# A decoder step on one Trainium2 core: order of the feed-forward groups, queue of the raw weight tiles, and order of VectorE's work at openings

## The reference, cut to what matters

```python
D_MODEL = 1024
D_FF = -(-8 * D_MODEL // (3 * 256)) * 256      # 2816

def swiglu(xn, w_gu, w_down):
    g, u = jnp.split(xn @ w_gu, 2, axis=-1)
    return (jax.nn.silu(g) * u) @ w_down

hp = hp + swiglu(rmsnorm(hp, g_ffn[l]), w_gu[l], w_down[l])
hs = hs + swiglu(rmsnorm(hs, g_ffn[l]), w_gu[l], w_down[l])
y_prompt = rmsnorm(hp, g_final)
```

## Time and profile before

| | us |
|---|---|
| median of three runs (lowest, highest) | 2819.61 (2816.98, 2821.58) |
| the profiled execution | 2815.63 |
| its span in the profile | 2813.8 |
| TensorE busy | 2749.6 (98%) |
| VectorE busy | 1560.3 (55%) |
| ScalarE busy | 1033.0 (37%) |
| GpSimd busy | 381.0 (14%) |

### The profile page before, as it was taken

One profiled execution on the slowest core, in us unless ns is written; L12 is line 12 of the kernel. 1 busy time (PEld: TensorE's weight loads), 2 busy tenths in 40 slices (PEclk: granted clock), 3 DMA queues, 4 the chain that ended last, 5 costly groups with the idle time before them and its releaser, 6 DMA issues.

```text
span 2813.8 us, 42434 instructions
## 1 busy us (share of the span) xinstructions
PE 2749.6 (98%) x16279; PEld 2630.7 (93%) x16279; DVE 1560.3 (55%) x3052; ACT 1033.0 (37%) x2222; POOL 381.0 (14%) x347
## 2 busy tenths in 40 slices
PE   8999999999999999999999999999999999999998
PEld 8788879999998999999899999999999999999998
DVE  6634653346545445545474886876555536656354
ACT  6543443233223344344343444453222323222223
POOL 2744530000000000000001330310000011000001
PEclk9999999999999999999999999999999999999999
DMA  7987759767976888798776667687664577755753
GB/s 265 353 332 280 284 189 335 259 252 268 334 303 254 328 331 313 284 376 316 284 274 243 249 239 282 242 300 247 225 240 171 196 252 274 260 198 173 254 184 116
DMA packets 203567, 742.82 MB, mean 264 GB/s; under 512 B 22732, under 2 KB 66956, under 8 KB 167144
## 3 DMA queue, kind: packets, MB, share of 16 engines
q1 hardware_dynamic: 180576, 671.25, 65.4%
q0 software_dynamic: 13392, 57.15, 5.5%
q10 hardware_dynamic: 9400, 11.72, 1.2%
HBM read 565.43 MB, written 174.61 MB: 263 GB/s over the span
## 4 chain that ended last, share of the span: by engine, by line
PE 86%; DVE 6%; DMA 3%; issue 2%; ACT 1%; POOL 1%; SPq 0%; ACTq 0%; DVEq 0%; POOLq 0%
PE gb L994 35%; PE gb L1387 11%; PE ta L1387 6%; PE tb L1387 5%; PE td L1387 4%; PE gb L1238 3%; PE gb L1423 3%; PE gm L1387 3%; PE ta L1238 2%; PE ta L1436 2%; PE gm L1423 1%; PE ta L1423 1%; PE td L1238 1%; POOL units L954 1%; PE tb L1436 1%
## 5 line engine op out<-in xcount | busy, mean ns | idle before, releaser
L994 PE MATMUL gb<-xn_hi,w_hl 128*128 128x384 f32 (+2 forms) x2280 | 646.0, 355 | 2.7 <-DVE big L2082 2.7
L994 PEld LDWEIGHTS gb<-xn_hi,w_hl 128*128 128x128 f32 x2280 | 419.9, 188 | 23.3 <-issue 3.3
L994 PE MATMUL gb<-xn_lo,w_hl 128*128 128x384 f32 (+2 forms) x1160 | 406.3, 350 | 0.0
L994 PE MATMUL gb<-act_hi,w_hl 128*128 128x384 f32 (+3 forms) x1424 | 379.1, 344 | 14.1 <-DVE w_hl L2051 10.2
L1387 PE MATMUL gb<-tq,units 128*128 128x342 f32 (+1 forms) x2052 | 347.8, 320 | 0.0
L1387 PEld LDWEIGHTS gb<-tq,units 128*128 128x128 f32 x2052 | 328.3, 189 | 0.0
L994 PEld LDWEIGHTS gb<-act_hi,w_hl 128*128 128x128 f32 x1424 | 259.4, 190 | 29.7 <-DVE w_hl L2051 10.5
L954 POOL TENSOR_TENSOR units<-wq,units 128x512 fp32r<-128x512 f32 (+1 forms) x92 | 116.7, 1289 | 1047.8 <-ACT units L1604 1047.8
L994 PE MATMUL gb<-act_lo,w_hl 128*128 128x384 f32 (+3 forms) x712 | 243.3, 342 | 0.0
L1604 ACT ACTIVATE units<-wq 128x512 fp32r<-128x512 f32 (+1 forms) x320 | 183.0, 606 | 163.9 <-DVE wq L2201 85.7
L994 PEld LDWEIGHTS gb<-xn_lo,w_hl 128*128 128x128 f32 x1160 | 218.2, 188 | 10.1 <-issue 0.2
(11 more groups left out here) (414 smaller groups left out, 4587.1 us busy)
## 6 DMA issues: line engine op xcount, KB each, us to landing
w_hl<-split_d SPq DMA_DIRECT2D x212, 1024.0 KB, 7.0
units<-kept_d SPq DMA_DIRECT2D x308, 512.0 KB, 4.7
kept_d<-units SPq DMA_DIRECT2D x154, 512.0 KB, 4.4
split_d<-w_hl SPq DMA_DIRECT2D x53, 1024.0 KB, 6.2
wq<-w_gu SPq DMA_DIRECT2D x44, 512.0 KB, 5.7
wq<-w_sp SPq DMA_DIRECT2D x44, 512.0 KB, 5.7
w_raw<-w_st SPq DMA_DIRECT2D x37, 512.0 KB, 6.9
w_raw<-w_kv SPq DMA_DIRECT2D x32, 512.0 KB, 5.8
```

The source lines that it names most:

```text
L994: mm = pe.matmul(bank[:, 0:wd], a[:, s, k * P:(k + 1) * P], r[:, k, 0:wd], start=(first and k == ks[0] and i == 0), stop=(last and k == ks ...
```

## The change

It has three parts.

1. `FFG` becomes [4, 4, 4, 4, 4, 2]: the group of two is now the last of each block, behind five groups of four. The fourth, fifth and sixth groups thereby change form in all blocks: there are 14 crossed groups in place of 11, and the last groups have two tiles.
2. `ffn_weights` is moved from SP's queue to GpSimd's. GpSimd waits for the low part that frees the entry and then issues the load. On this queue stand also the pooled low parts and the loads of the residual (`xf<-x_d`); the latter are moved to other steps of block 0. SP keeps the stores and loads of kept units, the operands and the outputs.
3. `prepared(u)`: in a crossed group the weight work of the opening is done two steps later, behind the additions, and caught up at the first two steps of the second half. Hidden low 1 stays at the first step, and hidden low 2 moves behind the additions of the third.

```diff
@@ -66,7 +66,7 @@
 FH = [w // 2 for w in FW]
 NFB = len(FW)
 NH = max(FH)
-FFG = [4, 4, 4, 2, 4, 4]
+FFG = [4, 4, 4, 4, 4, 2]
 NG = len(FFG)
 PRODUCTS = 7
 NU = 8
@@ -751,19 +751,6 @@
                 src = xn_d[k:k + 4, :, c0 + half * n:c0 + half * n + n].rearrange("k p c -> p k c")
                 sp.dma_start(tf[:, t, part, :, 0:n], src).then_inc(t_loaded[i], 16)
 
-            def ffn_weights(q):
...
             def keep_unit(u):
 
                 w = unit_width(u)
@@ -793,26 +780,15 @@
             sp.wait_ge(xn_stored, 32 * (NB - 1))
             for i in range(2, 4):
                 operand(0, i)
-            for q in range(3):
-                ffn_weights(q)
             split(G_ALL - 2)
             split(G_ALL - 1)
-            sp.wait_ge(pt_done, NB * 8)
-            ffn_weights(3)
             read_out(sp, G_ALL - 1)
             store_x(NB - 1, x_d, x_stored)
 
             for u, (b, gr, f, p) in enumerate(UNITS):
-                if fresh(u):
-                    if pooled(u):
-                        sp.wait_ge(unit_lo_p, LOW_P[u])
-                    else:
-                        sp.wait_ge(unit_lo_v, LOW_V[u])
-                        if f < CROSS:
-                            keep_unit(u)
-                    free = ENTRY[u] if f < 0 else {PRODUCTS - 2: ENTRY[u], PRODUCTS - 1: ENTRY[u] + 1}.get(POS[u])
-                    if free is not None and free + NQ in UNIT_OF:
-                        ffn_weights(free + NQ)
+                if b == 0 and 0 <= f < CROSS:
+                    sp.wait_ge(unit_lo_v, LOW_V[u])
+                    keep_unit(u)
                 if u + AHEAD < len(UNITS) and not fresh(u + AHEAD):
                     load_unit(u + AHEAD)
                 if (b, gr, f, POS[u]) == (0, 0, 2, 5):
@@ -932,27 +908,53 @@
                     pool.dma_start(xf[:, m:m + 4, half, 0:n],
                                    x_d[m:m + 4, :, c0 + half * n:c0 + half * n + n].rearrange("k p c -> p k c")).then_inc(xf_loaded[m // 4], 16)
 
+            def ffn_weights(q):
+
+                u, side = UNIT_OF[q]
+                b, gr, f, p = UNITS[u]
+                if f < 0:
+                    w = FFG[gr] * P
+                    pool.dma_start(raw_tile(q)[:, 0:w], w_dn[gr * KT + p, :, 0:w]).then_inc(raw_loaded[q % NQ], 16)
+                elif f >= CROSS:
+                    w = 2 * FFG[gr] * P
+                    pool.dma_start(raw_tile(q)[:, 0:w], w_sp[2 * (2 * gr + f - CROSS) + side, :, 0:w]).then_inc(raw_loaded[q % NQ], 16)
+                else:
+                    pool.dma_start(raw_tile(q), w_gu[2 * (sum(FFG[:gr]) + f) + side]).then_inc(raw_loaded[q % NQ], 16)
+
+            pool.wait_ge(dec_pe, PE_OUT)
+            for q in range(3):
+                ffn_weights(q)
+            pool.wait_ge(pt_done, NB * 8)
+            ffn_weights(3)
+
             for u, (b, gr, f, p) in enumerate(UNITS):
-                if gr == 0 and f == 2 and POS[u] == 0:
-                    if b:
-                        for m in (0, 4):
-                            pool.wait_ge(y_ready, 8 * b - 4 + m)
-                            store_y(b - 1, m)
-                        for m in (0, 4):
-                            pool.wait_ge(y_stored[m // 4], 32 * b)
-                            load_xf(b, m)
-                    else:
-                        pool.wait_ge(xn_stored, 32 * NB + 16)
-                        load_xf(b, 4)
-                if u == 0:
-                    pool.wait_ge(group_done, G_ALL)
-                    pool.wait_ge(x_stored, 32 * NB + 16)
-                    load_xf(0, 0)
+                if b and gr == 0 and f == 2 and POS[u] == 0:
+                    for m in (0, 4):
+                        pool.wait_ge(y_ready, 8 * b - 4 + m)
+                        store_y(b - 1, m)
+                    for m in (0, 4):
+                        pool.wait_ge(y_stored[m // 4], 32 * b)
+                        load_xf(b, m)
                 if pooled(u):
                     w = unit_width(u)
                     pool.wait_ge(unit_hi_done, HIGHS[u])
                     pool.tensor_tensor(units[:, u % NU, 1, 0:w], unit_source(u), units[:, u % NU, 0, 0:w].bitcast(F32),
                                        ALU.subtract).then_inc(unit_lo_p, 1)
+                if fresh(u):
+                    free = ENTRY[u] if f < 0 else {PRODUCTS - 2: ENTRY[u], PRODUCTS - 1: ENTRY[u] + 1}.get(POS[u])
+                    if free is not None and free + NQ in UNIT_OF:
+                        if pooled(u):
+                            pool.wait_ge(unit_lo_p, LOW_P[u])
+                        else:
+                            pool.wait_ge(unit_lo_v, LOW_V[u])
+                        ffn_weights(free + NQ)
+                if (b, gr, f, POS[u]) == (0, 0, 1, 1):
+                    pool.wait_ge(group_done, G_ALL)
+                    pool.wait_ge(x_stored, 32 * NB + 16)
+                    load_xf(0, 0)
+                if (b, gr, f, POS[u]) == (0, 0, 3, 6):
+                    pool.wait_ge(xn_stored, 32 * NB + 16)
+                    load_xf(0, 4)
 
         @block.tensor
         def _(pe):
@@ -2769,6 +2771,16 @@
                     if u + ahead < len(UNITS) and UNITS[u + ahead][2] >= 0 and fresh(u + ahead) and POS[u + ahead] == 0:
                         weight_sum(PAIR[u + ahead], i)
 
+            def prepared(u):
+
+                b, gr, f, _ = UNITS[u]
+                if f == CROSS + 1 and POS[u] < 2:
+                    return (u - 2, u - 1) if POS[u] == 0 else (u - 1, u)
+                if f == CROSS:
+                    return (u - 2,) if POS[u] else ()
+                opening = crossed(b, gr) and f == FFG[gr] - 1 and POS[u] == PRODUCTS - 1
+                return () if opening else (u,)
+
             for u, (b, gr, f, p) in enumerate(UNITS):
                 if f >= CROSS:
                     cross_step(u, b, gr, f - CROSS, p)
@@ -2790,13 +2802,10 @@
                             operand_low(b + 1, i)
                 if gr == 0 and f == 0 and POS[u] < (1 if b else 2):
                     operand_low(b, POS[u] + (6 if b else 5))
-                opening = crossed(b, gr) and f == FFG[gr] - 1 and POS[u] == PRODUCTS - 1
-                if not opening:
-                    if f == CROSS and POS[u] == 0:
-                        weights_of(u - 1)
-                        hidden_low(b, gr, FFG[gr] - 1, 1)
-                        hidden_low(b, gr, FFG[gr] - 1, 2)
-                    weights_of(u)
+                if f == CROSS and POS[u] in (0, 2):
+                    hidden_low(b, gr, FFG[gr] - 1, 1 + POS[u] // 2)
+                for w in prepared(u):
+                    weights_of(w)
                 if 0 <= f < CROSS and p == 5:
                     hidden_right(b, gr, f)
 
```

More of the change, by code:

```diff
@@ L752, in operand @@
                 sp.dma_start(tf[:, t, part, :, 0:n], src).then_inc(t_loaded[i], 16)
-            def ffn_weights(q):
-                u, side = UNIT_OF[q]
-                b, gr, f, p = UNITS[u]
-                if f < 0:
-                    w = FFG[gr] * P
-                    sp.dma_start(raw_tile(q)[:, 0:w], w_dn[gr * KT + p, :, 0:w]).then_inc(raw_loaded[q % NQ], 16)
-                elif f >= CROSS:
-                    w = 2 * FFG[gr] * P
-                    sp.dma_start(raw_tile(q)[:, 0:w], w_sp[2 * (2 * gr + f - CROSS) + side, :, 0:w]).then_inc(raw_loaded[q % NQ], 16)
-                else:
-                    sp.dma_start(raw_tile(q), w_gu[2 * (sum(FFG[:gr]) + f) + side]).then_inc(raw_loaded[q % NQ], 16)
             def keep_unit(u):
@@ L933, in load_xf @@
                                    x_d[m:m + 4, :, c0 + half * n:c0 + half * n + n].rearrange("k p c -> p k c")).then_inc(xf_loaded[m // 4], 16)
-            for u, (b, gr, f, p) in enumerate(UNITS):
-                if gr == 0 and f == 2 and POS[u] == 0:
-                    if b:
-                        for m in (0, 4):
-                            pool.wait_ge(y_ready, 8 * b - 4 + m)
-                            store_y(b - 1, m)
-                        for m in (0, 4):
-                            pool.wait_ge(y_stored[m // 4], 32 * b)
-                            load_xf(b, m)
-                    else:
-                        pool.wait_ge(xn_stored, 32 * NB + 16)
-                        load_xf(b, 4)
-                if u == 0:
-                    pool.wait_ge(group_done, G_ALL)
-                    pool.wait_ge(x_stored, 32 * NB + 16)
-                    load_xf(0, 0)
+            def ffn_weights(q):
[14 more added lines that the diff above has]
+            ffn_weights(3)
+            for u, (b, gr, f, p) in enumerate(UNITS):
+                if b and gr == 0 and f == 2 and POS[u] == 0:
[5 more added lines that the diff above has]
+                        load_xf(b, m)
                 if pooled(u):
```

## The result

| | before | changed |
|---|---|---|
| median of six runs, us | 2819.51 | 2840.51 |
| lowest and highest | 2816.54, 2821.58 | 2838.67, 2841.41 |
| the profiled execution | 2815.63 | 2841.41 |
| its span in the profile | 2813.8 | 2839.6 |

The changed kernel is slower: its ratio to before is 1.0076, 95% interval 1.0066 to 1.0086, 21 us. I had forecast no change (2820.3), and the range ended at 2833.

A forecast was written before the change was run, and what follows sets the result against it. TensorE was taken as the bound, DMA engines second in the first pairs alone. Order and openings +10.7 and queue -10 gave +0.7 us; against the median 2819.6 this meant 2820.3 us, range 2805 to 2833.

The forecast's parts named there:

- The order: All blocks, group of two last: with the openings, +8.9, +4.1 and -2.3 us in blocks 0, 1, 2, together +10.7.
- the ends: Last groups of blocks 0 and 1: VectorE becomes the bound, 28.2 us each; block 2 to the last sum, 23.7.
- the chain's 30.1 us: Ends of blocks 0 and 1: operand at 3.0 us plus VectorE's 27.0, 30.1 with semaphore; less 1.9 gives 28.2.
- The step on the operands' load: Ends of blocks 0 and 1: three fewer SP issues of 0.75 us, first made operand at 3.0 us, not 5.26.
- The openings: Start of crossed groups: 27.5 us in place of 28.5 in blocks 1 and 2, 28.9 for 29.1 in block 0.
- The queue: Raw tiles on GpSimd's queue: -10 us in the first group of block 0, with GpSimd's issuing hidden.
- the first group's part: First group of block 0: at most 15.4 us to be had; pairs gain about 4 to 5, down projection 5.
- I take 5 of its 6.7 us: First down projection of block 0: not in a jam (share 0.48) once the backlog is gone, gains 5 us.
- that is 6 us beside 16.07 of work in a stretch of 29, hidden: Crossed groups of block 0: at most 8 loads of 0.75 us, issued by GpSimd beside its own work, cost nothing.
- Due later in every case: GpSimd's queue: its low parts and the residual's loads behind a waiting raw load are needed later; no size given.
- The raw tiles land no sooner: Rival: first group keeps 99.9 us, total 2830.3; decided by raw tiles over 10 us in first pairs; chance 0.17.
- The clock falls at the ends: Rival, ends of blocks 0 and 1: TensorE's clock drops, some 4 us each, +8.7, total 2829 us; chance 0.11.

The follow-up runs named there:

- the lighter sums: Against the order part alone, VectorE's sums of squares at the ends of blocks 0 and 1 take an eighth of the columns: 2836.51 us.
- the changed kernel with the residual later: Against the changed kernel, the second residual loads are issued behind the first raw tiles of the down projection: 2830.66 us.

## Why the prediction was wrong, point by point

- **The order, right in mechanism, too low by 3 us.** Its terms with the old openings give 4 x 29.1 + 28.2 - 134.9, 5 x 28.5 + 28.2 - 161.6 and 5 x 28.5 + 23.7 - 163.5, together +21.5 us; measured +24.6. VectorE bounds the ends, as the lighter sums show. Too small were the ends: I took the next pair's first product off the chain's 30.1 us, but in the changed kernel that product itself starts 0.95 us late and the second starts at 31.4 us (1919.13 less 1887.78). That is 1.3 us at each end. Another 1.3 lies behind the last sum.
- **The step on the operands' load was wrong, and the number came out right by luck.** I said that the load would land at 3.0 us, since SP no longer issues raw tiles ahead of it. VectorE in the changed kernel:

```profile
1892.99 1.58 DVE L2235 TENSOR_TENSOR tf<-tf 128x1368 f32<-128x1368 f32 x1 [2.77 <-DMA tf<-xn_d]
```

 That is 5.2 us into the group, as before. SP does issue it earlier (5.5 us ahead of the group, before 3.4), but the four loads land after 8.5 us (median), before after 6.8; GpSimd's tiles are under way beside them, as above. What made up for it is a shorter chain behind it, 26.1 us to the last addition in place of 27.0.
- **The openings, right.** 27.5 us were worked out and 27.5 measured, with the wait for L2215 named (0.44 us on average for 0.7). In sum -8.4 us alone and -10.4 in the new order, for some -10.8.
- **The queue, the step that failed.** It was booked with -10 us and costs 6.7, so that the sum came out at no change and the kernel is 21 us slower. Of the first group's part, the pairs' 4.6 came. The sentence "I take 5 of its 6.7 us" failed for the first down projection: the position of the residual's loads directly ahead of the late tile, plain in the rows of GpSimd's order, was not priced. And "that is 6 us beside 16.07 of work in a stretch of 29, hidden" failed for block 0: I set the issue time against GpSimd's idle time of the window, but its low parts are a chain with VectorE's sums and ScalarE's high parts, and the loads between them lie on it. With the queue alone they cost 1.0 us per crossed group, and with the new openings on top 1.5 to 2.4 in the changed kernel, as the experiments show. This is 9 to 10 us over four groups against the forecast, and 1.7 for the pairs ahead of them. "Due later in every case", said of the low parts queued behind a load, failed with it. Taken with the first down projection this is 16 of the 20 us that were missing.
- **The rivals.** "The raw tiles land no sooner" named the result that is nearest to the measured one (2830.3, still 10 us short of it), for a wrong reason: its point of decision, over 10 us for a raw tile in the first pairs, was just missed (9.7 us), and without the residual's loads ahead of them the down projection's tiles land in 6.6 us. Of the two rules of the Trainium skill, page "DMA: Bandwidth & Descriptors", the one that the DMA engines take turns between the queues (section "SWDGE vs HWDGE vs iDMA") agrees with that row, since eight stores of SP's queue were issued in the same stretch. The one that all issuers share the same 16 engines (section "Issuing engines are not separate DMA queues") agrees with the operands' load, which got slower with GpSimd's tiles beside it. What that section adds, that another issuer saves only the issuing time, is not what the first pairs show: a raw tile landed after 9.7 us in place of 13.4, and the pairs got 4.6 us shorter. "The clock falls at the ends" happened (0.94 and 0.82 in the windows), but the length of an end does not follow it: 28.3 us at 0.94 in the changed kernel, 27.7 at 0.82 with the order alone, and the lighter sums shortened the end at a clock of 0.93. Its sum had a slip besides: 2819.6 and 8.7 are 2828.3 us, not 2829.

## What to carry to other kernels

An in-order queue with idle time is no free place for a load: what counts is whether work that someone waits for stands behind it, and each load has to be priced at its place, with what is queued directly ahead of it and behind it. Taking a part of the matmuls off TensorE brings nothing where the other engine's work per tile stays; here the new order has 72 matmuls fewer, an estimated 11.5 us of TensorE, and alone it made the kernel 24.6 us slower. When a change has several parts, measure them apart: here one was worth 8 us, one cost 25, and the third had a gain of 9 in it that its own remainder ate up.

## What the runs showed of the hardware that was not expected

The same wait of 2.0 us was followed in some groups by twelve matmuls at half speed and in others by none, within one execution (31.54 and 30.65 us, the first two crossed groups of the changed kernel with the residual later). The operands' load didn't become faster when SP's other tiles left its queue: from its first issue to its use it needed 10.7 us with GpSimd's tiles beside it, and 8.6 before with SP's own tiles between. And one and the same sum of VectorE (128x512) took 0.68 us with GpSimd at rest and 1.70 to 1.79 us beside a low part of GpSimd; its additions from a bank of TensorE took 0.50 us in either case.
